# Attention of a two-layer network: turns and products in batches of two groups, with VectorE moving every second group of the selected part

## The chip, the cores and the metric

The kernel runs on one core of a Trainium2 chip. The metric is the time of one execution on the device, in microseconds (us). A core has five engines, each with its own instruction queue, which it works off strictly in order: TensorE (PE; its weight loads are shown as PEld), VectorE (DVE), ScalarE (ACT), GpSimd (POOL) and SyncE (SP). They are tied together by semaphores.

## The reference, cut to what matters

The network has two layers; each is a mixer and a feed-forward block with a convolution. The change touches the mixer of the second layer alone, an attention of 1024 queries and 16 heads of 64 in two groups of keys and values. Each query attends in three ways and the results are added with gates:

```python
s_c = q_blk . k_cmp - slopes * dist_c          
p_c = masked_softmax(s_c, dist_c >= 0)
o_c = p_c . v_cmp
imp = p_c . cover                              # importance of each block of 64 keys
_, top = lax.top_k(imp, 6)                     # first, own and previous block are forced
s_s = q_blk . k_sel[top] - slopes * dist_s     # selected blocks
o_s = masked_softmax(s_s, dist_s >= 0) . v_sel[top]
s_w = q_blk . k_win - slopes * dist_w          # the last 512 keys
o_w = masked_softmax(s_w, valid_w) . v_win
o = g[0] * o_c + g[1] * o_s + g[2] * o_w
```

## The kernel before, in words

The attention is one list, `steps`, of 144 steps (lines 117 to 135). A step is a part (2 compressed, 1 window, 0 selected), a head and a tile of 128 queries. A compressed step does eight heads at once. A window or selected step does two heads against `tiles` tiles of 128 keys: at most 5 in the window, up to 8 in the selected part, where all keys up to the query's tile are scored and the blocks that were not chosen are masked. The first 80 steps are compressed and window steps mixed (16 compressed); they are called the first part. The last 64 steps, from `SELECTED` on, are the selected part. They come in eight couples (two groups of keys, four couples each) of a large and a small query tile: 8 and 1 tiles of keys, 7 and 2, 6 and 3, 5 and 4. Within a couple a wide step and a narrow one take turns, four pairs to a couple.

A step goes through these stages; the names in brackets are the functions:

- TensorE multiplies queries and keys (`scores`, line 1693, matmuls at 1701 and 1711) into PSUM banks 0 to 3. There is room for the scores of one step only, so it first waits until VectorE has read those of the step before (`neg_ready`).
- VectorE adds the mask and slope and takes the extreme (`bias_step`, line 1310, one pass for each of the two heads); compressed steps have their own chain of small operations (`cmp_front`, `cmp_back`).
- ScalarE takes the exponential and its sum (`exp_step`, line 859), VectorE the reciprocal (`norm_step`, line 1321), and GpSimd multiplies by reciprocal and gate (`scale_step`, line 607; semaphore `scaled`).
- TensorE turns the probabilities, block by block of 128 x 128, into bank 4 or 5 (`turn`, line 1735). Up to four blocks, 512 columns, are a group; groups are numbered through all steps (`pair_groups`), 176 in the first part and 160 in the selected part, and group g uses bank 4 + g % 2. A wide and a narrow step have five groups together.
- A group is copied from PSUM into one of five buffers PTR (semaphores `pt_sb` for ScalarE, line 873, and `pt_sv` for VectorE, line 1347).
- TensorE multiplies it with the values (`values`, lines 1748 and 1754) into bank 6 or 7, and VectorE adds the result to the output (`out_step`, lines 1333 and 1335).

The order is fixed by these loops. For step p TensorE first issues the scores of step p + AHEAD, then turns the groups of p one by one, and after each turn of g issues the products of g - LAG; with LAG = 3 and AHEAD = 3 turns and products alternate. VectorE does, for step p, the bias of step p + 3, the reciprocals of step p + 2, and then in `evacuate(p)` goes through the groups of p: copies those that `by_vector` gives it (none before), and does the output sum of a step whose last group is g - LAG. ScalarE does, for step p, the exponentials of step p + 2 and then copies the groups of p. A turn of g waits until group g - 2 has been copied out of its bank:

```python
def turn(g):
    ...
    if g >= 2:
        evacuated(g - 2)
```

The copies by VectorE are written in both kernels; only `by_vector` decides whether there are any:

```python
if by_vector(g):
    w = min(4, tiles - 4 * i) * P
    dve.wait_ge(tr_done, g + 1)
    dve.wait_ge(pv_done, g - len(PTR) + 1)
    dve.tensor_copy(PTR[g % len(PTR)][:, 0:w], PS[:, 4 + g % 2, 0:w]).then_inc(pt_sv, 1)
if ends(g - LAG):
    out_step(group_step[g - LAG])
```

## Time and profile before

| what | before |
|---|---|
| median of three runs | 3404.81 us (3403.2 to 3405.83) |
| the profiled execution | 3404.87 us |
| its span, first to last instruction | 3403.1 us |
| mean granted clock of TensorE | 0.949 |
| TensorE busy | 3063.8 us, 90% |
| GpSimd busy | 1469.3 us, 43% |
| VectorE busy | 1354.4 us, 40% |
| ScalarE busy | 944.9 us, 28% |

The times of a profiled execution are read from the start of its span. Each engine's busy time is what its instructions took; idle time in front of an instruction is given in brackets with the instruction that ended it, or with "issue" where the profile shows nothing that was waited for. A line such as L1735 is a line of the kernel. In the timeline, instructions of one kind that follow each other are merged into one row with their count; a matmul of two passes counts twice, so four products of 64 x 128 appear as x8. The granted clock is the share of TensorE's full clock of 2.4 GHz; 0.50 is 1.2 GHz.

### The profile page before, as it was taken

The page shows a single profiled execution, that of the slowest core. Times are in us where ns is not written, and L with a number is a line of the kernel's source. Part 1 is how long each engine was busy: PE and PEld are TensorE (multiplying, and loading weights), DVE is VectorE, ACT ScalarE, POOL GpSimd, SP SyncE. Part 2 cuts the span into 40 slices and gives each one's busy share as a digit, 9 for nine tenths or more (in the row PEclk, how much of TensorE's full clock was granted, in tenths as well). Part 3 has the DMA queues.
Part 4 walks back from the last instruction along what each step waited for, and adds up shares of the span by engine and source line. Part 5 has one row for each costly group of instructions (what it writes and reads, how often), then busy time and mean ns, then how long its engine had stood idle before and what let it go on. Part 6 is the DMA issues. An engine that isn't in the chain of part 4 may idle for free. (4 is left out here: it accounts for less than half of the span.)

```text
span 3403.1 us, 41503 instructions
## 1 busy us (share of the span) xinstructions
PE 3063.8 (90%) x16565; PEld 2424.3 (71%) x16565; DVE 1354.4 (40%) x1910; ACT 944.9 (28%) x1447; POOL 1469.3 (43%) x910
## 2 busy tenths in 40 slices
PE   5967888977989999999899698889879899999998
PEld 4747887764778888888777465555557688888887
DVE  3675445353333223133300477654342332231334
ACT  3332223222033112012101264667661331120121
POOL 4324433374554444444543243344444544444442
PEclk8988999998999999999899797999989899999999
DMA  3100000110111111111112200000001111111111
GB/s 134 44 25 1 1 1 26 49 50 25 48 33 49 47 46 48 51 49 46 43 44 54 79 2 1 1 1 2 1 13 44 32 49 49 49 48 45 49 46 71
DMA packets 211542, 127.43 MB, mean 37 GB/s; under 512 B 8905, under 2 KB 208078, under 8 KB 211150
## 3 DMA queue, kind: packets, MB, share of 16 engines
q1 hardware_dynamic: 209600, 125.25, 12.5%
q8 instruction: 96, 1.57, 0.2%
q10 hardware_dynamic: 1805, 0.28, 0.0%
q14 instruction: 41, 0.33, 0.0%
HBM read 112.94 MB, written 8.39 MB: 36 GB/s over the span
## 5 line engine op out<-in xcount | busy, mean ns | idle before, releaser
L437 POOL TENSOR_TENSOR WH<-WR,ONES 128x1024 fp32r<-128x1024 f32 (+1 forms) x194 | 459.6, 2369 | 1224.5 <-PE PS L1398 1200.7
L1398 PE MATMUL PS<-YH,WH 128*128 128x512 f32 x2336 | 739.0, 398 | 77.3 <-POOL YL L462 34.7
L1398 PE MATMUL PS<-YL,WH 128*128 128x512 f32 x2336 | 727.2, 393 | 0.0
L1398 PE MATMUL PS<-YH,WL 128*128 128x512 f32 x2336 | 725.5, 392 | 0.0
L1398 PEld LDWEIGHTS PS<-YH,WH 128*128 128x128 f32 x2336 | 441.3, 190 | 192.2 <-issue 53.7
L1398 PEld LDWEIGHTS PS<-YL,WH 128*128 128x128 f32 x2336 | 444.6, 190 | 93.7
L1398 PEld LDWEIGHTS PS<-YH,WL 128*128 128x128 f32 x2336 | 442.6, 189 | 93.2
L440 POOL TENSOR_TENSOR WL<-WR,WH 128x1024 fp32r<-128x1024 f32 (+1 forms) x194 | 482.1, 2485 | 15.2
L1170 DVE SCALAR_TENSOR_TENSOR X<-PS,PTF,X 128x1023 f32<-128x1023 f32 (+1 forms) x176 | 225.7, 1282 | 573.5 <-ACT X L818 560.7
L818 ACT ACTIVATE X<-PS,PTF 128x1024 f32<-128x1024 f32 x88 | 106.2, 1207 | 840.4 <-PE PS L1398 840.2
L873 ACT ACTIVATE Z<-PS 128x512 f32<-128x512 f32 (+2 forms) x336 | 182.6, 545 | 191.6 <-PE PS L1735 189.9
L1398 PE MATMUL PS<-MH,WH 128*128 128x512 f32 x704 | 217.3, 390 | 0.0
L1398 PE MATMUL PS<-MH,WL 128*128 128x512 f32 x704 | 216.9, 389 | 0.0
L1398 PE MATMUL PS<-ML,WH 128*128 128x512 f32 x704 | 216.7, 389 | 0.0
L1711 PE MATMUL PS<-X 64*128 64x512 f32 (+3 forms) x768 | 157.9, 518 | 54.8 <-DVE STAT L1310 54.1
L607 POOL TENSOR_SCALAR X<-X,STAT,SM 128x640 f32<-128x640 f32 (+7 forms) x171 | 135.4, 801 | 144.2 <-DVE STAT L1321 144.2
L1754 PE MATMUL PS<-Z,X 128*64 128x128 f32 x2112 | 188.3, 295 | 9.0 <-DVE Z L1335 9.0
L1754 PEld LDWEIGHTS PS<-Z,X 128*64 128x64 f32 x2112 | 113.3, 140 | 62.4 <-issue 59.5
L1735 PE MATMUL PS<-IDENT,X 128*128 128x128 f32 (+1 forms) x799 | 155.9, 300 | 0.3 <-POOL X L599 0.2
L1398 PEld LDWEIGHTS PS<-MH,WH 128*128 128x128 f32 x704 | 131.9, 188 | 28.9 <-DVE ML L1179 1.6
L1398 PEld LDWEIGHTS PS<-MH,WL 128*128 128x128 f32 x704 | 132.2, 188 | 27.4
L1398 PEld LDWEIGHTS PS<-ML,WH 128*128 128x128 f32 x704 | 132.2, 188 | 27.4
(315 smaller groups left out, 3522.4 us busy)
## 6 DMA issues: line engine op xcount, KB each, us to landing
WR<-in_ffn_w_up_dram SPq DMA_DIRECT2D x88, 512.0 KB, 3.8
WR<-in_hy_w_in_dram SPq DMA_DIRECT2D x28, 512.0 KB, 3.8
WR<-in_ffn_w_down_dram SPq DMA_DIRECT2D x32, 448.0 KB, 3.6
WR<-in_ffn_w_down_dram SPq DMA_DIRECT2D x16, 512.0 KB, 3.8
WR<-in_nsa_w_in_dram SPq DMA_DIRECT2D x14, 512.0 KB, 3.7
Z<-in_x_dram SPq DMA_DIRECT2D x8, 512.0 KB, 7.3
xt_scratch<-H SPq DMA_DIRECT2D x1, 4096.0 KB, 12.1
H<-xt_scratch SPq DMA_DIRECT2D x1, 4096.0 KB, 12.2
```

Of the source, the lines that this page charges most:

```text
L437: pool.tensor_tensor(WH[:, slot, 0:k, :], WR[:, slot, 0:k, :], ONES[:, :].unsqueeze(1).broadcast_to([P, k, P]), ALU.mult).then_inc(w_hi, 1)
L440: pool.tensor_tensor(WL[:, slot, 0:k, :], WR[:, slot, 0:k, :], WH[:, slot, 0:k, :].bitcast(f32), ALU.subtract).then_inc(w_split, 1)
L607: pool.tensor_scalar(score_buf(p, i, 0, w), score_buf(p, i, 0, w), STAT[:, 2, n % 8:n % 8 + 1], GATE[:, qt, gate:gate + 1], ALU.mult, ALU. ...
L818: act.activation(X[:, 16 + s, :], gemm_ps(s), ACT.Identity, scale=PTF[:, bass.ds(j + tap, 1)], bias=PTF[:, bass.ds(j + (C_FBIAS + l * 2 * ...
L873: act.activation(PTR[g % len(PTR)][0:rows, 0:w], PS[0:rows, 4 + g % 2, 0:w], ACT.Copy).then_inc(pt_sb, 1)
L1170: dve.scalar_tensor_tensor(out=X[:, 16 + s, d:], in0=gemm_ps(s)[:, 0:SEQ - d], scalar=PTF[:, bass.ds(j + tap, 1)], in1=X[:, 16 + s, d:], o ...
L1398: ins = pe.matmul(PS[:, 2 * slot + a, :], w[:, slot, i, :], y[:, i, a * HALF:(a + 1) * HALF], start=(i == 0 and w is WH and y is hi), stop ...
L1711: ins = pe.matmul(gemm_ps(i)[:, a:e], X[part, h // 2, chunk(qt)], X[part, kt, first * P + a:first * P + e], start=True, stop=True)
L1735: ins = pe.transpose(PS[0:rows, 4 + g % 2, (k - 4 * i) * P:(k - 4 * i + 1) * P], src, IDENT[:, :])
L1754: ins = pe.matmul(PS[head_part(k), 6 + p % 2, 0:P], X[:, (VS, VW)[b], (first + t) * P + (h // JH) * DH:(first + t) * P + (h // JH) * DH + DH],
```

## The change

```diff
--- before.py
+++ after.py
@@ -145,7 +145,7 @@
         for b_, h_, qt_ in steps:
             pair_groups.append(pair_groups[-1] + (2 if b_ == 2 else (2 * keys_of(qt_, b_)[1] + 3) // 4))
 
-        LAG, AHEAD = 3, 3
+        BATCH, LAG, AHEAD = 2, 2, 3
 
         score_at, scores_free = [], []
         ring, at_ = 0, 0
@@ -173,7 +173,7 @@
         group_step = [p_ for p_ in range(len(steps)) for _ in range(pair_groups[p_], pair_groups[p_ + 1])]
 
         def by_vector(g):
-            return False
+            return group_step[g] >= SELECTED and g % BATCH == 1
 
         n_vector = [sum(by_vector(k) for k in range(g)) for g in range(len(group_step) + 1)]
 
@@ -1759,15 +1759,17 @@
             pe.wait_ge(kv_sb, 2)
             for p in range(AHEAD):
                 scores(p)
-            for p in range(len(steps)):
-                if p + AHEAD < len(steps):
-                    scores(p + AHEAD)
-                for g in range(pair_groups[p], pair_groups[p + 1]):
-                    turn(g)
-                    if g >= LAG:
+            for g0 in range(0, pair_groups[-1] + LAG, BATCH):
+                batch = range(g0, g0 + BATCH)
+                for g in batch:
+                    if g in pair_groups and g < pair_groups[-1] and group_step[g] + AHEAD < len(steps):
+                        scores(group_step[g] + AHEAD)
+                for g in batch:
+                    if g < pair_groups[-1]:
+                        turn(g)
+                for g in batch:
+                    if 0 <= g - LAG < pair_groups[-1]:
                         values(g - LAG)
-            for g in range(pair_groups[-1] - LAG, pair_groups[-1]):
-                values(g)
             pe.wait_ge(y_ready2, MT)
             units(U_NOUT, MT)
             ffn(1, 3, 4 * MT)
```

Three things change. TensorE works in batches of two groups: in a batch it issues the scores of every step that falls due, then both turns, then the products of the two groups before (LAG is 2 now). If both groups of a batch begin a step, two steps' scores stand one after the other at its start. VectorE's output sums stand one group earlier in its queue. And in the selected part VectorE copies the odd groups, 80 of 160, while ScalarE keeps the even ones and all of the first part.

The first place is TensorE in the selected part, in the second kind of couple (7 and 2 tiles of keys). L1711 are scores, L1735 turns of one block each, L1754 products. Before:

```order
L1711 MATMUL PS<-X 128x512 x2
L1711 MATMUL PS<-X 128x384 x2
L1735 MATMUL PS<-IDENT,SRX 128x128 x2
L1754 MATMUL PS<-Z,X 64x128 x4
L1711 MATMUL PS<-X 128x256 x2
L1735 MATMUL PS<-IDENT,SRX 128x128 x4
L1754 MATMUL PS<-Z,X 64x128 x4
L1735 MATMUL PS<-IDENT,SRX 128x128 x4
L1754 MATMUL PS<-Z,X 64x128 x4
L1735 MATMUL PS<-IDENT,SRX 128x128 x4
L1754 MATMUL PS<-Z,X 64x128 x2
```

The same place with the change:

```order
L1711 MATMUL PS<-X 128x512 x2
L1711 MATMUL PS<-X 128x384 x2
L1711 MATMUL PS<-X 128x256 x2
L1735 MATMUL PS<-IDENT,X 128x128 x8
L1754 MATMUL PS<-Z,X 64x128 x6
L1735 MATMUL PS<-IDENT,X 128x128 x8
L1754 MATMUL PS<-Z,X 64x128 x8
L1711 MATMUL PS<-X 128x512 x2
L1711 MATMUL PS<-X 128x384 x2
```

The scores of the wide step (512 and 384 columns) and of the narrow one (256) now stand side by side with no turn or product between them, eight turns come in a row, and then six products.

The second place is VectorE in the selected part, in the first kind of couple (8 and 1 tiles). L1310 is the bias pass, L1321 the reciprocals, L1335 the output sum. Before:

```order
L1310 ISA SRX,STAT<-PS,Z 128x1024 [waits att_sc_ready]
L1310 ISA STAT 128x1
L1321 RECIPROCAL STAT<-STAT 128x2 [waits att_p_ready]
L1310 ISA SRX,STAT<-PS,Z 128x128 [waits att_sc_ready,att_tr_done,att_selb_ready]
L1310 ISA STAT 128x1
L1310 ISA SRX,STAT<-PS,Z 128x128 [waits att_sc_ready]
L1310 ISA STAT 128x1
L1321 RECIPROCAL STAT<-STAT 128x2 [waits att_p_ready]
L1335 TENSOR_TENSOR Z<-Z,PS 128x128 [waits att_o_used,att_pv_done] x2
L1310 ISA X,STAT<-PS,Z 128x1024 [waits att_sc_ready,att_tr_done,att_selb_ready]
```

The same place with the change, where L1347 is the copy of a group:

```order
L1310 ISA SRX,STAT<-PS,Z 128x1024 [waits att_sc_ready]
L1310 ISA STAT 128x1
L1321 RECIPROCAL STAT<-STAT 128x2 [waits att_p_ready]
L1310 ISA SRX,STAT<-PS,Z 128x128 [waits att_sc_ready,att_tr_done,att_selb_ready]
L1310 ISA STAT 128x1
L1310 ISA SRX,STAT<-PS,Z 128x128 [waits att_sc_ready]
L1310 ISA STAT 128x1
L1321 RECIPROCAL STAT<-STAT 128x2 [waits att_p_ready]
L1347 COPY Z<-PS 128x512 [waits att_pv_done,att_tr_done]
L1335 TENSOR_TENSOR Z<-Z,PS 128x128 [waits att_o_used,att_pv_done] x2
L1347 COPY Z<-PS 128x512 [waits att_pv_done,att_tr_done]
```

The first copy stands behind the narrow step's bias and behind reciprocals that wait for ScalarE's exponentials (`att_p_ready`), the second behind two output sums that wait for products (`att_pv_done`).

## Rows read from the trace of the kernel before

**Rows 1.** The profile's page, busy time and share of the span.

```profile
PE 3063.8 (90%) x16565; PEld 2424.3 (71%) x16565; DVE 1354.4 (40%) x1910; ACT 944.9 (28%) x1447; POOL 1469.3 (43%) x910
```

**Rows 2.** Stretches: us, busy time (instructions) by engine, granted clock, DMA share, GB/s.

```profile
1925.00:2050.00 125.00, 116.13 (x1058) 76.48 (x1058) 89.11 (x248) 79.85 (x184) 56.73 (x70) 0.96 0.01 1
2050.00:2135.00 85.00, 69.70 (x496) 45.36 (x494) 60.83 (x139) 35.50 (x83) 27.11 (x31) 0.74 0.00 1
```

**Rows 3.** Timeline, fifth couple: start, length (us), engine, line, work, [idle before <- releaser].

```profile
2401.31 1.99 PE L1711 MATMUL PS<-X 64*128 64x512 f32 x8
...
2403.47 1.23 DVE L1310 CUSTOM_DVE_ANT_0 SRX<-PS,Z 128x1024 f32<-128x1024 f32 x1 [2.93 <-PE PS L1711]
...
2404.74 1.15 ACT L859 ACTIVATE SRX<-SRX,STAT 128x1024 f32<-128x1024 f32 x1 [0.65 <-DVE STAT L1310]
...
2405.90 0.49 PE L1711 MATMUL PS<-X 64*128 64x128 f32 x4 [1.64 <-DVE STAT L1310]
...
2406.32 0.66 PE L1735 MATMUL PS<-IDENT,X 128*128 128x128 f32 x4
...
2407.16 0.17 DVE L1321 RECIPROCAL STAT<-STAT 128x2 f32<-128x2 f32 x1
...
2410.80 1.56 PE L1711 MATMUL PS<-X 64*128 64x512 f32 x6
```

**Rows 4.** Waits, selected part: who waits for whom, us in total, times, longest.

```profile
PEld PS L1711 <- DVE STAT L1310: 26.8, 24, 1.9
```

**Rows 5.** Timeline, third couple, TensorE's matmuls.

```profile
2335.08 0.66 PE L1735 MATMUL PS<-IDENT,X 128*128 128x128 f32 x4
2335.66 0.44 PE L1754 MATMUL PS<-Z,X 128*64 128x128 f32 x4
2336.03 0.66 PE L1735 MATMUL PS<-IDENT,X 128*128 128x128 f32 x4
```

**Rows 6.** Timeline, the last products: TensorE's weight loads.

```profile
2526.66 1.51 PEld L1754 LDWEIGHTS PS<-Z,X 128*64 128x64 f32 x28 [0.17 <-issue]
```

**Rows 7.** Groups by shape, VectorE: xcount | busy us, mean ns | idle before.

```profile
L1262 DVE COPY Z<-PS 128x512 f32<-128x512 f32 x15 | 10.4, 690 | 12.5 <-PE PS L1748 12.3
```

**Rows 8.** Groups by shape, ScalarE, selected part.

```profile
L873 ACT ACTIVATE Z<-PS 128x512 f32<-128x512 f32 x134 | 79.5, 596 | 68.7 <-PE PS L1735 68.5
```

**Rows 9.** Chain of waits: start, length (us), what; one wide step's scores a row.

```profile
2320.76 1.54 PE PS L1711 x8
...
2337.28 1.49 PE PS L1711 x8
...
2352.84 1.28 PE PS L1711 x8
...
2488.66 1.28 PE PS L1711 x8
...
2503.99 1.28 PE PS L1711 x8
```

**Rows 10.** Timeline, first part, TensorE's matmuls.

```profile
1965.40 1.35 PE L1711 MATMUL PS<-X 64*128 64x512 f32 x8
...
1973.30 0.70 PE L1711 MATMUL PS<-X 64*128 64x256 f32 x4 [1.22 <-DVE STAT L1310]
...
1995.15 1.35 PE L1711 MATMUL PS<-X 64*128 64x512 f32 x8
```

**Rows 11.** Timeline, first and second couple, TensorE's matmuls.

```profile
2262.51 1.99 PE L1711 MATMUL PS<-X 64*128 64x512 f32 x8
...
2273.49 1.99 PE L1711 MATMUL PS<-X 64*128 64x512 f32 x8
...
2284.47 1.77 PE L1711 MATMUL PS<-X 64*128 64x512 f32 x8
...
2288.58 0.70 PE L1711 MATMUL PS<-X 64*128 64x256 f32 x4 [1.38 <-DVE STAT L1310]
```

**Rows 12.** Stretches of two us, first couple.

```profile
2270.00:2272.00 2.00, 2.00 (x14) 1.34 (x14) 0.29 (x1) 0.50 (x2) 0.99 (x1) 0.50 0.00 0
```


## The prediction

> **What bounds the kernel now.** I read the page first, then busy time by stretches, the waits and the chain of the attention, and last the timeline, engine by engine. TensorE is busy for 90% of the span [rows 1]. The change acts only on the attention's loop, from 1925 to 2530 us. Its first part (compressed and window steps) lasts to 2246 us, the selected part to 2530 us. In the first part TensorE is near full at the whole clock, and at a mean clock of 0.74 in the 85 us where VectorE ranks the blocks [rows 2]. In the selected part TensorE works steadily and waits for one thing: its next scores stand behind VectorE's passes over the last ones, 26.8 us in all [rows 4]. The fifth couple shows how. Wide scores start at 2401.31 us, VectorE reads them in two passes, and the narrow scores start at 2405.90 us, 4.59 us after the wide ones; 1.64 us of that was idle [rows 3]. The next pair starts 9.49 us after the first.
>
> **What the change removes.** A turn of four blocks takes 0.58 us to the start of the products, products of two blocks 0.37 us [rows 5]. In the tail 28 product loads run without a break in 1.51 us, 0.054 each, so four blocks (8 loads) cost 0.43 us [rows 6]. The rest, 0.15 us, is paid once whenever TensorE goes from turns to products, to scores, or back; the tail's row has 0.17 us of it as idle of the weight loads. A satisfied wait costs nothing visible: that tail passes three groups. Counted over the whole listing of TensorE's instructions, changes of kind fall from 427 to 247 before the first selected turn and from 379 to 211 after it: 348 times 0.155 us is 54 us at most.
>
> This meets a rule that speaks against the change. The Trainium skill, TensorE: Matmul & The Clock Gate, section Step-by-step: what each phase is for, says that the load of the next weights is pulled ahead of running matmuls; by it a change of kind would cost nothing, the saving would be nil, and only the added waits would be left. The trace disagrees, with 0.17 us of idle at each change; the Trainium skill, TensorEngine Tiling (Array Packing), Key Properties, says that changing the tiling mode drains the engine, and that fits.
>
> **What it costs, selected part.** Per step pair there are a wide step (W0, W1, ...) and a narrow one (N...), five groups in all, so batches repeat every two pairs: 5 batches, 10 groups, 36 blocks turned and multiplied. 80 of the 160 groups are now moved by VectorE, 64 of them with 512 columns. Such a copy took 0.69 us from PSUM [rows 7] against ScalarE's 0.60 [rows 8]: about 50 us more for VectorE, which idles for over half of this part. Its length is covered; its place in the queue is not. VectorE copies a step's odd groups only after the bias passes of the step three ahead, the reciprocals of the step two ahead (which wait for ScalarE's exponentials), and the output sum of a step just ended, which waits for its products.
>
> First and fifth couple, eight pairs, wide 8 tiles, narrow 1. Work of two pairs without waits: scores 2 x (1.91 + 0.42), taken from start to start; blocks 72 x 0.1075 = 7.74; ten changes 1.55; together 13.95 us. The waits, with t=0 at the start of the wide scores in the batch that holds N and the next W0:
> - Both scores are now issued at once, so narrow scores start at 4.59 as before [rows 3], with nothing between: 2.68 us idle.
> - N and W0 are turned by 5.8 us. N is even, so ScalarE copies it first (to 5.8) and only then takes the two exponentials of the wide step; from the start of the first to VectorE's reciprocal it was 2.42 us [rows 3], so the reciprocal comes at 8.25. W0's copy stands behind it: done at 9.0. TensorE has done products of four blocks each twice (to 6.8) and the turn of W1 (7.4); the turn of W2 needs W0's bank: 1.6 us idle.
> - In the other batch with wide scores, a turn pair (0.80) and a product pair (1.01) lie between: 4.59 - 1.91 - 1.81 = 0.87 idle. Where the output sum stands ahead of a copy, another 0.3.
> Sum 19.4 us, against 2 x 9.49 = 19.0: longer by 0.45.
> Second and sixth couple, eight pairs (7 and 2 tiles): the same work; narrow scores could start 4.11 us after wide ones of 1.70 [rows 11], so the waits are 2.4, 1.8 (N is four blocks, ScalarE starts later), 0.6 and 0.05: 18.9 against 18.15 (four pairs from 2284.47 [rows 11] to 2320.76 us [rows 9], halved): longer by 0.8.
> Third and seventh (6 and 3 tiles), no two scores in one batch: work 13.7, waits 0.1 and 0.3 for scores, and 1.1 for W0's copy, which now stands behind the output sum of the last wide step, the narrow bias and the reciprocals; with two of 0.1 it is 15.45 against 15.56 [rows 9]. Fourth and eighth (5 and 4): 13.55 + 1.35 + 0.15 = 15.05 against 15.33 [rows 9].
> Each couple kind has four such double pairs: 4 x (0.45 + 0.8 - 0.1 - 0.3) = +3.4 us. Of 26 us of saved changes here nothing is left. Ends: no wait for copies at all, -22 us (the 1.9, 1.85, 1.3 and 1.4 us of them, four times); each of them 0.5 us longer, +12.
>
> **First part.** All copies stay with ScalarE. A cycle of one compressed, two window steps of 5 tiles and a narrow one takes 14.9 us (two in 29.75) with a wait of 1.22 us before the narrow scores [rows 10]. It has nine groups, so nine changes go, 1.4 us. Of the new order I followed two cycles: 24.9 us of work; 1.7 and 1.9 us for narrow scores, since VectorE's work on the compressed step lies ahead of the second wide bias; 0.1 to 0.4 for copies behind exponentials: 28.6 against 29.75, 0.6 less a cycle. Ten cycles at the full clock give 6 us, the rest of the part, where VectorE's ranking or the lower clock rules, 0 to 7, and I take 2: -8 us. Ends: 0, and all 180 changes, -28. The tail (two groups of products fewer) and the start are taken as nothing.
>
> Sum: 3404.87 (profiled; median 3404.81) + 3.4 - 8 = 3400.3, say 3401 us. A measurement of this kernel can tell about 0.2% (6.8 us) from no change; this is inside it.
>
> **The rivals.**
> - The copies come in time. If VectorE's queue is freer than I walked it, the 26 us of its copy waits in the selected part shrink. For it: VectorE was under half busy there; against: the queue is in order, and the wide exponentials of 2.4 us cannot be hidden by 1.6 us of work. Three quarters gone: 3400 - 19 = 3381 us. The Trainium skill, TensorEngine Tiling (Array Packing), PSUM Bottleneck, advises ScalarE and VectorE together for emptying PSUM; by it this rival is the natural outcome.
> - The longer single waits pull TensorE's clock. In the first couple a wait of 1.64 us was followed by a stretch at 0.50 of the clock (1.2 GHz) [rows 12], and that pair took 10.98 us [rows 11] against 9.49: 1.5 us. In the fifth couple the same wait did nothing. Now eight double pairs have waits of 2.4 to 2.7 and then 1.6 to 1.8 us. If each drops it, 8 x 1.5 = 12 us more, less the some 3 us already paid in the first couple, with 3 more in the first part: 3401 + 12 = 3413 us. It decides from about half of them on.
> - The change does nothing: no; the listing shows the batches and 80 copies.
>
> **How the numbers follow.** Forecast 0.45 (it reaches about 8 us to either side: faster 0.12, same 0.30, slower 0.03), copies in time 0.30 (faster), clock 0.25 (same 0.08, slower 0.17). Faster 0.42, same 0.38, slower 0.20. The range takes in the middle of the first rival and the second's whole: 3382 to 3414.
>
> **What would show it.** Wide scores followed at once by narrow ones, with idle of 2.4 to 2.7 us for VectorE's STAT in the first, second, fifth and sixth couples; TensorE's turns (line 1735 of before) waiting 1 to 2 us for VectorE's copy, about 20 us in all, where they waited for no copy; fewer 0.17 us idles; double pairs of 19.4, 18.9, 15.4 and 15.1 us; the first part about 8 us shorter. It is wrong if turns wait for VectorE's copy for under 10 us, if the first part moves by over 15 us, or if the clock of the four slow couples falls below 0.85.

## The result, and the profile after

| what | before | after |
|---|---|---|
| median of six runs each, same chip | 3405.61 us | 3419.99 us (3419.49 to 3421.83) |
| the profiled execution | 3404.87 us | 3419.88 us |
| its span | 3403.1 us | 3418.1 us |
| mean granted clock of TensorE | 0.949 | 0.948 |

The ratio after to before is 1.0046, 95% interval 1.0035 to 1.0056. The change made the kernel slower by 14 us. The forecast was 3401 us with a range of 3382 to 3414, so the result lies outside it, on the slower side.

The busy times of the kernel after, to be read against [rows 1]:

```profile
PE 3032.7 (89%) x16565; PEld 2438.5 (71%) x16565; DVE 1397.8 (41%) x1990; ACT 890.1 (26%) x1367; POOL 1470.3 (43%) x910
```

VectorE has its 80 copies (1990 instructions against 1910) and 43 us more work, ScalarE 80 fewer and 55 us less. TensorE has the same 16565 matmuls and 31 us less busy time, in a program that is 15 us longer: what grew is idle time of TensorE.

The length of the selected part, from VectorE's first bias of 1024 columns to the first operation of ScalarE on the attention's sum (line 883), went from 280.6 us (2248.22 to 2528.79) to 296.7 us (2246.24 to 2542.95). The first part, from 1925 us to that bias, went from 323.2 to 321.2 us. So the selected part lost 16.1 us, the first part gained 2.0, and these two nearly make up the difference of the profiled executions.

The table sets the eight couples of the selected part side by side, from wide bias to wide bias: length in us, and the mean granted clock behind the stroke.

| couple | 1 | 2 | 3 | 4 | 5 | 6 | 7 | 8 |
|---|---|---|---|---|---|---|---|---|
| before | 38.2 / 0.91 | 36.0 / 1.00 | 31.9 / 1.00 | 31.5 / 1.00 | 36.4 / 1.00 | 36.0 / 1.00 | 31.9 / 1.00 | 38.7 / 1.00 |
| after | 36.0 / 1.00 | 40.6 / 0.92 | 34.0 / 0.95 | 32.3 / 1.00 | 41.6 / 0.92 | 38.8 / 0.96 | 33.9 / 0.95 | 39.5 / 1.00 |

**The waits.** These are the waits of the selected part in the kernel after: us in total, times, longest. The first row answers to [rows 4].

```profile
PEld PS L1711 <- DVE STAT L1310: 43.5, 32, 3.4
...
PE PS L1711 <- DVE STAT L1310: 32.9, 28, 2.6
...
PEld PS L1735 <- issue: 27.1, 66, 0.8
PEld PS L1735 <- DVE Z L1347: 22.1, 23, 2.2
...
PE PS L1735 <- DVE Z L1347: 16.5, 18, 1.9
...
DVE STAT L1321 <- ACT SRX L859: 12.2, 7, 2.4
...
DVE STAT L1321 <- ACT X L859: 8.3, 5, 2.3
```

The same wait has a row of the weight loads (PEld) and one of the matmuls (PE); the first is the larger, and the two are not to be added. Of the kernel before the matmuls' row for the maximum is

```profile
PE PS L1711 <- DVE STAT L1310: 21.3, 20, 1.6
```

Sums of waits below are those of the weight loads where nothing else is said; waits read from a timeline of TensorE's matmuls are the matmuls'. Scores wait for VectorE's maximum 43.5 us, against 26.8 us before. Turns now wait 22.1 us for VectorE's copy (line 1347), of which there was none before. The "issue" idle in front of turns, in which the changes of kind lie, is 27.1 us in 66 places; before it was 41.5 us in 141. In front of products it went from 27.8 us (162) to 12.7 us (76).

**One double pair.** This is the timeline of the fifth couple in the kernel after, TensorE and VectorE, to be read against [rows 3]:

```profile
2408.55 1.99 PE L1711 MATMUL PS<-X 64*128 64x512 f32 x8
2410.70 1.23 DVE L1310 CUSTOM_DVE_ANT_0 SRX<-PS,Z 128x1024 f32<-128x1024 f32 x1 [2.38 <-PE PS L1711]
...
2413.14 0.49 PE L1711 MATMUL PS<-X 64*128 64x128 f32 x4 [2.60 <-DVE STAT L1310]
2413.56 1.17 PE L1735 MATMUL PS<-IDENT,X 128*128 128x128 f32 x6
...
2414.66 1.98 PE L1754 MATMUL PS<-Z,X 128*64 128x128 f32 x16
...
2416.71 0.17 DVE L1321 RECIPROCAL STAT<-STAT 128x2 f32<-128x2 f32 x1 [2.07 <-ACT X L859]
2416.79 0.69 DVE L1347 COPY Z<-PS 128x512 f32<-128x512 f32 x1
...
2421.64 1.23 DVE L1310 CUSTOM_DVE_ANT_0 X<-PS,Z 128x1024 f32<-128x1024 f32 x1 [2.14 <-PE PS L1735]
...
2424.07 0.49 PE L1711 MATMUL PS<-X 64*128 64x128 f32 x4 [1.32 <-DVE STAT L1310]
```

The narrow scores start 4.59 us after the wide ones, as forecast, with 2.60 us of idle in front, since nothing stands between. The two turns of the batch (six blocks) end by 2414.7 us, but the copy of the second starts at 2416.79 us: VectorE stood 2.07 us at a reciprocal that waited for ScalarE's exponentials. And at 2421.64 us a thing is to be seen that the forecast didn't have: VectorE starts a wide bias only when TensorE has done turns (its releaser is line 1735, not 1711), because the buffer it writes is still being turned. The narrow scores behind it wait 1.32 us instead of the 0.87 us forecast.

TensorE's clock around that wait, in stretches of two us (columns as in [rows 2]):

```profile
2413.00:2415.00 2.00, 1.86 (x14) 1.41 (x16) 0.67 (x7) 0.97 (x2) 0.88 (x2) 0.75 0.00 0
2415.00:2417.00 2.00, 2.00 (x18) 1.67 (x15) 0.29 (x2) 1.67 (x4) 0.03 (x1) 0.50 0.00 0
2417.00:2419.00 2.00, 2.00 (x22) 1.41 (x20) 1.06 (x4) 0.60 (x1) 2.00 (x2) 0.90 0.00 0
```

Behind the wait of 2.60 us about 3.4 us passed at half the clock (1.2 GHz): (0.25 + 0.50 + 0.10) x 2 us x 2. The products in it, sixteen rows, took 1.98 us, and 1.09 us at the full clock seven us later.

The chain of waits of the kernel after gives the wide scores of the fifth to eighth couples, one row each, to be read against [rows 9]:

```profile
2398.65 2.82 PE PS L1711 x8
...
2419.00 1.92 PE PS L1711 x8
...
2439.02 1.70 PE PS L1711 x8
...
2458.92 1.70 PE PS L1711 x8
...
2478.54 1.49 PE PS L1711 x8
...
2495.14 1.54 PE PS L1711 x8
...
2511.34 1.28 PE PS L1711 x8
...
2527.08 1.28 PE PS L1711 x8
```

Double pairs took 20.35, 19.90, 16.60 and 15.74 us; forecast were 19.4, 18.9, 15.45 and 15.05.

**The first part.** Compressed scores (line 1701) mark its cycles. First before, then after, TensorE's timeline:

```profile
1930.42 1.25 PE L1701 MATMUL PS<-X 64*128 64x63 f32 x16
...
1990.81 1.11 PE L1701 MATMUL PS<-X 64*128 64x63 f32 x16
...
2139.51 1.11 PE L1701 MATMUL PS<-X 64*128 64x63 f32 x16
...
2169.03 1.11 PE L1701 MATMUL PS<-X 64*128 64x63 f32 x16
```

```profile
1928.54 1.46 PE L1701 MATMUL PS<-X 64*128 64x63 f32 x16
...
1958.69 0.80 PE L1711 MATMUL PS<-X 64*128 64x128 f32 x4 [4.17 <-DVE STAT L1310]
...
1996.23 1.11 PE L1701 MATMUL PS<-X 64*128 64x63 f32 x16
...
2133.26 1.11 PE L1701 MATMUL PS<-X 64*128 64x63 f32 x16
...
2166.69 1.11 PE L1701 MATMUL PS<-X 64*128 64x63 f32 x16
```

The first five intervals between compressed scores took 60.4 us before and 67.7 after, the next eight 148.7 and 137.0, the last two 29.5 and 33.4. So the middle gained 11.7 us and the two ends lost 11.2. The loss at the start has a wait of 4.17 us. The scores of a wide and of a narrow window step stand side by side there, and VectorE has its operations on a compressed step (lines 1243 to 1249) ahead of the wide bias. The kernel before had 0.64 us in front of the same narrow scores. The granted clock tells the same: from 1925 to 1985 us it was 0.92 before and is 0.82 now, from 2135 to 2200 us it was 1.00 and is 0.92, and from 2050 to 2135 us it rose from 0.74 to 0.82.

### The profile page after: what moved, and what is told of

It is laid out like the page before. It is cut to its first block, busy times and chain, and to the rows that moved or that the text cites. A ratio compares the mean times of both kernels' runs of the same rounds, so it can differ in the third digit from the quotient of the medians.

```text
span 3418.1 us, 41503 instructions
## 1 busy us (share of the span) xinstructions
PE 3032.7 (89%) x16565; PEld 2438.5 (71%) x16565; DVE 1397.8 (41%) x1990; ACT 890.1 (26%) x1367; POOL 1470.3 (43%) x910
## 3 DMA queue, kind: packets, MB, share of 16 engines
q1 hardware_dynamic: 209600, 125.25, 12.4%
## 4 chain that ended last, share of the span: by engine, by line
PE 74%; DVE 15%; ACT 3%; POOL 3%; issue 2%; DMA 1%; SPq 0%; ACTq 0%; DVEq 0%; POOLq 0%
PE PS L1398 55%; PE PS L1711 4%; PE PS L1735 3%; PE PS L1476 3%; PE PS L1754 2%; DVE X L1310 2%; DVE H L962 2%; POOL YL L462 1%; DVE X L947 1%; PE PS L1534 1%; DVE SRX L1310 1%; DVE X L910 1%; DVE X L1074 1%; DVE X L924 1%; POOL YL L531 1%
## 5 line engine op out<-in xcount | busy, mean ns | idle before, releaser
L440 POOL TENSOR_TENSOR WL<-WR,WH 128x1024 fp32r<-128x1024 f32 (+1 forms) x194 | 482.0, 2485 | 15.2
L1711 PE MATMUL PS<-X 64*128 64x512 f32 (+3 forms) x768 | 160.8, 526 | 86.3 <-DVE STAT L1310 82.4
L607 POOL TENSOR_SCALAR X<-X,STAT,SM 128x640 f32<-128x640 f32 (+7 forms) x171 | 135.6, 802 | 167.5 <-DVE STAT L1321 167.5
L873 ACT ACTIVATE Z<-PS 128x512 f32<-128x512 f32 (+2 forms) x256 | 132.9, 539 | 268.8 <-PE PS L1735 267.8
L1711 PEld LDWEIGHTS PS<-X 64*128 64x128 f32 x768 | 68.5, 200 | 151.4 <-DVE STAT L1310 100.9
L1754 PE MATMUL PS<-Z,X 128*64 128x128 f32 x2112 | 160.5, 292 | 5.1 <-DVE Z L1262 2.3
L1735 PE MATMUL PS<-IDENT,X 128*128 128x128 f32 (+1 forms) x799 | 140.2, 298 | 12.7 <-DVE Z L1347 11.5
```

The costliest lines, as they stand in the source:

```text
L440: pool.tensor_tensor(WL[:, slot, 0:k, :], WR[:, slot, 0:k, :], WH[:, slot, 0:k, :].bitcast(f32), ALU.subtract).then_inc(w_split, 1)
L607: pool.tensor_scalar(score_buf(p, i, 0, w), score_buf(p, i, 0, w), STAT[:, 2, n % 8:n % 8 + 1], GATE[:, qt, gate:gate + 1], ALU.mult, ALU. ...
L873: act.activation(PTR[g % len(PTR)][0:rows, 0:w], PS[0:rows, 4 + g % 2, 0:w], ACT.Copy).then_inc(pt_sb, 1)
L1711: ins = pe.matmul(gemm_ps(i)[:, a:e], X[part, h // 2, chunk(qt)], X[part, kt, first * P + a:first * P + e], start=True, stop=True)
L1735: ins = pe.transpose(PS[0:rows, 4 + g % 2, (k - 4 * i) * P:(k - 4 * i + 1) * P], src, IDENT[:, :])
L1754: ins = pe.matmul(PS[head_part(k), 6 + p % 2, 0:P], X[:, (VS, VW)[b], (first + t) * P + (h // JH) * DH:(first + t) * P + (h // JH) * DH + DH],
```

## The experiments

The theory after the result: the saving of changes of kind is real, and is given back by two things, (a) scores of two steps side by side, and (b) VectorE's copies behind the rest of its queue. The rival: the falls of TensorE's clock behind the longer single waits take the time. Times are medians of 4 to 10 executions, ratios are to the kernel before on the same chip with their 95% interval. Lengths of parts and waits are those of one profiled execution each; in experiments 4 and 12 that execution was about 4 us shorter than the median.

**1. The batches alone, ScalarE copies everything.**

```diff
 def by_vector(g):
-    return group_step[g] >= SELECTED and g % BATCH == 1
+    return False
```

> The changed kernel, but ScalarE copies every group. Theory A (VectorE's copies stand behind its bias passes, reciprocals and output sums, and TensorE's turns wait for them): the 38.7 us of waits for VectorE's copy go, ScalarE's copies wait behind exponentials instead, since in a batch the copy of the second group has 2.0 us and the wide exponentials alone take 2.3: some 20 to 30 us of waits for ScalarE. Time 3410 to 3420 us. Rival B (VectorE as such was the fault and ScalarE has room): under 3400 us. Rival C (ScalarE is the worse place): over 3425 us.

Measured: 3407.82 us, 1.0010 (1.0001 to 1.0020). Selected part 284.5 us. Of the change's 14 us, 12 go with VectorE's copies, more than the 10 us at most that were expected. What is left is still no gain: the waits for the maximum stay at 43.1 us, and waits for ScalarE's copies have taken the place of VectorE's 22.1 us:

```profile
PEld PS L1735 <- ACT Z L873: 19.7, 24, 1.8
```

So the 12 us can't be read from the row of the copies: turns wait for ScalarE nearly as long as for VectorE. In the account below idle fell by 9.1 us, 6.2 of it in the "issue" rows, for which the trace names no reason, and the time at half clock went from 24 to 14 us. (The expectation's 38.7 us of waits for VectorE's copy comes out only if the 22.1 us of the weight loads and the 16.5 of the matmuls are added, which counts the same waits twice; so with the 39 us in the expectation of experiment 5.)

**2. VectorE's copies alone**, in the kernel before, without batches.

```diff
 def by_vector(g):
-    return False
+    return group_step[g] >= SELECTED and g % 2 == 1
```

> The kernel before, its order of turns and products kept, with VectorE copying every odd group of the selected part. Theory A: with turns and products in alternation a copy has longer before its bank is wanted, but the first odd group of a wide step still stands behind bias, reciprocals and exponentials; some waits for the copy, selected part longer by 0 to 8 us: 3403 to 3413 us. Rival B (the copies by themselves make the whole loss): 3418 us or more. Rival C (the loss comes from the batches alone): within 2 us of the kernel before.

Measured: 3406.83 us, 1.0009 (0.9999 to 1.0019). Selected part 284.5 us in its profile, waits for line 1347 of 4.7 us in front of turns and 3.2 in front of products. The same copies that cost 12 us in batches cost 2 to 3 here, hardly to be told from none. That the copies have less room in batches, where two turns follow each other and the batch after needs both banks at once, fits this and is argued only.

**3. LAG of 2 alone**, in the kernel before.

```diff
-LAG, AHEAD = 3, 3
+LAG, AHEAD = 2, 3
```

> The kernel before with products two groups behind the turn instead of three, nothing else. Every theory: the number of changes of kind stays, VectorE's output sums stand one group earlier. I expect no difference above 2 us; if it is slower by over 5 us, the smaller distance and not the batch makes part of the loss.

Measured: 3407.28 us, 1.0006 (0.9996 to 1.0015); selected part 281.0 us. The smaller lag costs nothing that can be told from none.

**4. The second step's scores behind the first turn.** In the kernel after, the loops over a batch for scores and for turns are made one.

```diff
 for g in batch:
     if g in pair_groups and g < pair_groups[-1] and group_step[g] + AHEAD < len(steps):
         scores(group_step[g] + AHEAD)
-for g in batch:
     if g < pair_groups[-1]:
         turn(g)
```

> The changed kernel, but the scores of a batch's second step stand after the turn of its first group, not beside the other scores. Theory A (adjacent scores leave TensorE idle for all of VectorE's two passes and delay the turn, ScalarE's copy and the exponentials behind it): N is turned 2.7 us earlier, ScalarE starts its exponentials earlier, and of each double pair of the first, second, fifth and sixth couples 1 to 2.5 us come back, with three more changes of kind; 8 double pairs: 8 to 16 us, time 3404 to 3412 us. If the clock follows the length of a single wait (theory C) its falls in these couples go as well. Rival B (the waits for VectorE's copies alone matter): no change over 3 us.

Measured: 3400.15 us, 0.9985 (0.9975 to 0.9994). Selected part 278.4 us against 296.7. One turn between the two scores gives back 20 us, more than the 8 to 16 expected. The idle in front of the narrow scores of the fifth couple is 2.23 us instead of 2.60: the turn fills only a part of it, but it is done that much earlier, and its copy and the next exponentials with it. In all, waits for the maximum fell to 32.2 us and those for VectorE's copy to 17.3.

**5. Copies ahead of the reciprocals.** In the kernel after, VectorE goes through a step's groups first in the selected part, and takes the reciprocals of the step two ahead behind them.

```diff
-if p + AHEAD - 1 < len(steps):
+if p + AHEAD - 1 < len(steps) and p < SELECTED:
     norm_step(p + AHEAD - 1)
...
+if p >= SELECTED and p + AHEAD - 1 < len(steps):
+    norm_step(p + AHEAD - 1)
```

> The changed kernel, but in the selected part VectorE takes a step's copies and output sums before the reciprocals of the step two ahead, so no copy stands behind an exponential. Theory A (the copy waits behind the reciprocals, which wait for ScalarE's exponentials): the waits for VectorE's copy fall from 39 us to under 20, 1 to 1.5 us less a double pair, 16 of them: 3395 to 3408 us. Rival B (the copy is held by the output sum and the bias, not by the reciprocals): under 4 us of gain. Against both, the reciprocals now come later and GpSimd's scaling with them; if turns then wait for GpSimd it is no faster or slower.

Measured: 3405.50 us, 0.9998 (0.9989 to 1.0008). Selected part 278.7 us. Nothing but the place of one small instruction a step (0.16 us) was changed, and all of the change's 14 us came back. The waits of its selected part (line numbers are two higher below the edit):

```profile
PEld PS L1737 <- DVE Z L1347: 11.5, 14, 1.5
```

Half of the 22.1 us are gone, and of the 20.5 us that VectorE's reciprocals stood waiting for exponentials in the kernel after 0.2 are left. So about half of the lateness of VectorE's copy came from the reciprocal in front of it, and not from VectorE's speed. A part of the gain may be the clock's: only two falls were left in the selected part, of seven, though all eight waits of 2.07 to 2.60 us in front of narrow scores were still there, and idle fell by 13.0 us where the part became 18.0 shorter. No run separates the two.

**6. TensorE kept busy between adjacent scores.** In the kernel after, ten needless products of 128 x 128 stand between the two scores of a batch, in a bank that is free; they compute nothing that is used.

```diff
+due = [g for g in batch if ...]
+for g in due:
+    scores(group_step[g] + AHEAD)
+    if len(due) == 2 and g == due[0] and group_step[g] >= SELECTED:
+        evacuated(g0 - 2)
+        for _ in range(10):
+            pe.matmul(PS[:, 4 + g0 % 2, 0:P], IDENT[:, :], IDENT[:, :], start=True, stop=True)
```

> The changed kernel with ten needless 128 x 128 products between adjacent scores of the selected part, in the idle time of 2.4 to 2.7 us there, written to the bank of turned blocks that is free then. Nothing waits less. Theory C (a single long wait lowers TensorE's clock and the stretch at half clock behind it is dear): the falls in the first, second, fifth and sixth couples go, 5 to 7 of them at 1.5 to 1.9 us: 3407 to 3412 us, clock 1.00 in all those couples. Rival (the waits themselves are the whole loss): 3419 to 3421 us. If ten products are too long for the gap, later by up to 0.5 us a double pair: the trace shows the next scores' wait gone.

Measured: 3417.79 us, 1.0034 (1.0023 to 1.0046). In all eight couples the granted clock was 1.00, so the falls were taken away whole, and the selected part was 292.3 us long, 4.4 less. The narrow scores of the fifth couple still start 4.59 us after the wide ones, so the needless products delay nothing there. By the ratios the kernel gained 4 us and by the medians 2, and the two intervals overlap. The clock explains about 4 us of what the change lost there, and by the intervals not more than some 9. That is less than the 8 to 13 us expected if the clock were dear, and more than the nothing expected if the waits were all. Why it is not more is seen in the timeline of the fifth couple, kept busy:

```profile
2409.27 0.88 PE L1735 MATMUL PS<-IDENT,X 128*128 128x128 f32 x6
2410.07 1.09 PE L1754 MATMUL PS<-Z,X 128*64 128x128 f32 x16
2411.10 0.66 PE L1735 MATMUL PS<-IDENT,X 128*128 128x128 f32 x4
2413.24 0.66 PE L1735 MATMUL PS<-IDENT,X 128*128 128x128 f32 x4 [1.49 <-DVE Z L1347]
```

At the full clock turns and products are done sooner (the products in 1.09 us instead of 1.98), and then the next turn waits 1.49 us for VectorE's copy. By the weight loads it is 1.72 us, where the same turn had 0.26 in the kernel after. Summed over the selected part that wait grew from 22.1 to 27.8 us. In this pair most of what the half clock had cost was time that would have passed in a wait anyway. The clock of the first part, at half for 73 us in the kernel after and for 64 before, was not touched by this run.

**7. Both cures: scores apart, ScalarE copies everything.** The edits of experiments 4 and 1.

> Scores apart as in e4_scores_apart (3400.2 us), but ScalarE copies every group. With adjacent scores the same step from VectorE to ScalarE gave 12 us. If those 12 us were VectorE's place in the queue in general, it gives as much here: about 3388 us. If they came from adjacent scores plus clock falls that are gone here already, 3396 to 3402 us. Over 3404 us would mean that ScalarE's exponentials now hold the copies more than VectorE's queue did.

Measured: 3389.58 us, 0.9946 (0.9927 to 0.9965). Selected part 266.6 us, 14.0 less than in the kernel before. This is the 3388 us that was expected if the 12 us were VectorE's place in the queue in general. The two costs nearly add: VectorE's copies cost 12 us with adjacent scores (experiment 1) and 11 with the scores apart (from 3400.15), adjacent scores 20 us (experiment 4) and 18 (from 3407.82). Without both the batches do gain.

**8. Scores apart, copies by VectorE ahead of the reciprocals.** The edits of experiments 4 and 5.

> Scores apart and, in the selected part, VectorE's copies ahead of the reciprocals. Theory A: the 17 us of waits for VectorE's copies in e4_scores_apart fall by half or more: 3388 to 3396 us, the best of all. Rival: the reciprocals are late for GpSimd and TensorE's turns wait for the scaling instead: 3400 us or more.

Measured: 3397.68 us, 0.9977 (0.9968 to 0.9987). Selected part 277.2 us; waits for line 1347 fell only from 17.3 to 14.4 us. The move that gave 14 us beside adjacent scores gives 2.5 here. The time lies between the two expectations. With the turn between the scores the reciprocals in front of a copy hold it for far less already: VectorE stood 2.4 us at them in experiment 4, against 20.5 in the kernel after. Copies by VectorE still stand behind bias passes and output sums, and cost 8 us against ScalarE's (experiment 7). That these two are what holds them is argued from the queue; no run moved them.

**9. Second scores at the end of the batch**, ScalarE copies everything.

```diff
+for g in due[:1]:
+    scores(group_step[g] + AHEAD)
 for g in batch:
     ...
         turn(g)
 for g in batch:
     ...
         values(g - LAG)
+for g in due[1:]:
+    scores(group_step[g] + AHEAD)
```

> Batches of two, copies all on ScalarE, and the scores of a batch's second step stand behind both products of the batch instead of behind its turns' end. Against the kernel with ScalarE's copies and the scores apart, 3389.6 us (0.9946 of the kernel before). Theory 1 (what the batch lost came from adjacent scores only, and any work between the two scores cures it): two turns and two products now stand between a batch's scores, the waits for the maximum in the selected part fall from about 32 us to 15 or less, and the time is 3380 to 3389 us, 0.992 to 0.9945. Rival 2 (the loop bias, maximum, exponentials, normalising, copy sets the pace once scores come late): later scores make the exponentials and so the next turn late; the waits of products for copies or of turns for normalised values grow by as much, and the time is 3390 to 3410 us.

Measured: 3385.10 us, 0.9930 (0.9911 to 0.9948). Selected part 263.8 us; the narrow scores of the fifth couple wait 0.77 us. Waits for the maximum fell to 25.5 us and not to the 15 expected, and waits for ScalarE's copies grew (20.0 us in all against 10.5). The time is the first theory's, the growth of those waits the rival's: more work between the scores is better, but the loop through copy and exponentials takes part of it back.

**10. Experiment 7 with LAG 3.**

```diff
-BATCH, LAG, AHEAD = 2, 2, 3
+BATCH, LAG, AHEAD = 2, 3, 3
```

> The kernel with batches, ScalarE's copies and the second scores behind the first turn (3389.6 us, 0.9946 of the kernel before), with the scores three steps ahead of the products instead of what it had. Theory 1 (what is left in it are the turns' changes of kind and the copies, about 10 us of waits for ScalarE's copies in the selected part): a larger lead of the scores moves no copy earlier relative to its product, the copies' waits stay, and the time is within 3 us of 3389.6. Rival 2 (the 32 us of waits for the maximum are what is left): with more work between a step's scores and its exponentials they fall below 20 us and the time is 3380 to 3386 us.

Measured: 3402.71 us, 0.9992 (0.9983 to 1.0002), 13 us slower than experiment 7. Both expectations missed it. (The expectation's opening speaks of scores three steps ahead; what was changed is LAG, the products three groups behind the turns instead of two.) The waits of its selected part:

```profile
DVE Z L1335 <- PE PS L1754: 80.4, 51, 5.2
...
PEld PS L1711 <- DVE STAT L1310: 39.3, 32, 2.5
```

Experiment 7 had 52.3 us in the first of these rows and 31.8 in the second. The timeline of the third couple with LAG 3 shows how they are tied:

```profile
2335.55 1.56 PE L1711 MATMUL PS<-X 64*128 64x512 f32 x8
...
2338.34 0.29 DVE L1335 TENSOR_TENSOR Z<-Z,PS 128x128 f32<-128x128 f32 x1 [2.97 <-PE PS L1754]
2338.54 0.95 DVE L1310 CUSTOM_DVE_ANT_0 X<-PS,Z 128x768 f32<-128x768 f32 x1
...
2340.44 0.92 PE L1711 MATMUL PS<-X 64*128 64x384 f32 x4 [1.34 <-DVE STAT L1310]
```

The scores are done by 2337.2 us. VectorE stands at an output sum that waits for a product one group later than with LAG 2, and starts the bias 1.3 us late; the next scores wait 1.34 us for it. In experiment 7 the same scores (at 2333.47 us there) wait for nothing. LAG 2 alone was worth nothing (experiment 3); in batches it is worth 13 us. It is part of what makes them pay. Only half of it is seen here: the selected part is 6.6 us longer than in experiment 7 and the first part 6.3, which was not followed up.

**11. Second scores between turns and products**, ScalarE copies everything. As experiment 9, with the loop over `due[1:]` ahead of the products.

> Batches of two, ScalarE copies everything, and the second scores of a batch stand between its turns and its products. Neighbours: adjacent scores 3407.8 (1.0010 of the kernel before), second scores behind the first turn 3389.6 (0.9946), behind turns and products 3385.1 (0.9930). Theory 1 (it counts how much work stands between the two scores, and whether the copy of the turned groups is reached in time): both turns stand between, 0.8 to 1.1 us against a wait of about 2.7, and the copies of the batch get the scores as further cover; the waits for the maximum in the selected part are near 30 us, those for ScalarE's copies below 10, and the time is 3384 to 3391 us. Rival 2 (scores that come behind the turns make VectorE's bias wait for the turns, as in the kernel where they stand last, which had 33 us of such waits, and this sets the time): as much of such waits and 3388 to 3400 us.

Measured: 3378.96 us, 0.9915 (0.9897 to 0.9933), 27 us below the kernel before and 41 below the change, and the fastest of all; better than either theory expected. Selected part 266.3 us, first part 310.9. The page's busy times:

```profile
PE 3016.2 (89%) x16565; PEld 2429.5 (72%) x16565; DVE 1354.5 (40%) x1910; ACT 925.7 (27%) x1447; POOL 1470.7 (44%) x910
```

and the waits of its selected part:

```profile
PEld PS L1711 <- DVE STAT L1310: 32.8, 32, 2.0
...
DVE X L1310 <- PE PS L1735: 25.6, 12, 3.2
```

The second row is the one of the rival: the waits of VectorE's bias for turns are there, as large as in experiment 1 (26.1 us), and the kernel is 29 us faster all the same. Such a wait marks a bias that comes late, but it isn't what the adjacent scores cost. The selected part is as in experiment 7; the further gain is in the first part, where the eight cycles in the middle took 135.6 us and the last two 28.1 (1993.83, 2129.44 and 2157.56 us are the starts), and the clock of 2135 to 2200 us was 0.97 against 0.92 in the kernel after.

**12. The change in the first part alone**, single groups with LAG 2 behind it, ScalarE copies everything.

```diff
+whole = range(g0, g0 + BATCH)
+for batch in ([whole] if g0 < pair_groups[SELECTED] else [[g] for g in whole]):
```

> The change in the first part alone: batches of two before the selected part, single groups with LAG 2 behind it, ScalarE copies everything. Theory 1 (the change's loss arises in the selected part, its first part gains 2 us by the stage lengths read from the two traces; LAG 2 alone in the selected part costs nothing that can be told from none, 1.0006): first part 319 to 323 us long, selected part 280 to 283, time within 3 us of the kernel before (0.999 to 1.001). Rival 2 (the first part's gain of 8 us was real and is given back at the border or by the lower clock that the selected part's waits leave behind): 3395 to 3399 us, 0.997 to 0.9985.

Measured: 3402.90 us, 0.9988 (0.9979 to 0.9998), with a first part of 319.7 us and a selected part of 277.7 in its profile (323.2 and 280.6 in the kernel before). That is 3 us of gain by the medians and 4 by the ratio, with an interval that ends at 7. The time is nearer to the first theory than to the rival's 3395 to 3399, the ratio lies between them; the forecast's 8 us are just excluded.

**The account.** For each kernel the length of the selected part and what TensorE's weight loads stood idle for in it, us. The last column also has the "issue" idle in front of scores, 20 to 21 us in every row.

| kernel | length | maximum | copies | "issue", turns and products | all idle |
|---|---|---|---|---|---|
| before | 280.6 | 26.8 | 2.7 | 69.3 | 120.1 |
| after | 296.7 | 43.5 | 24.1 | 39.8 | 128.0 |
| 1 ScalarE copies | 284.5 | 43.1 | 22.4 | 33.6 | 118.9 |
| 4 scores apart | 278.4 | 32.2 | 17.9 | 43.9 | 114.2 |
| 5 copies first | 278.7 | 43.5 | 12.4 | 39.2 | 115.0 |
| 7 apart, ScalarE | 266.6 | 31.8 | 10.5 | 39.6 | 102.1 |
| 9 scores last | 263.8 | 25.5 | 20.0 | 35.7 | 101.8 |
| 10 LAG 3 | 273.2 | 39.3 | 4.5 | 44.8 | 108.4 |
| 11 between | 266.3 | 32.8 | 14.8 | 36.3 | 103.9 |

From before to experiment 7 idle fell by 18.0 us and the part by 14.0; from before to after idle rose by 7.9 and the part by 16.1. For the kernel after, the rest can be work at the lower clock: by the table of couples it spent 23 us at half clock (2 x (1 - clock) x length, summed) and the kernel before 7, which is at most 8 us of work done slower. For experiment 7, with 10 us at half clock, that gives less than 2 of the 4 us; the others are not traced. The count of falls differs between the runs too: seven in the kernel after, four, three and two in experiments 1, 4 and 5. What share of the gains of these three is the clock's isn't separated; experiment 6, with all seven gone, bounds it.

## Why the prediction was wrong

- **The saving of changes of kind** was right. Forecast for the selected part were 26 us; the "issue" idle in front of turns and products fell by 29.5 us over 161 fewer places, 0.18 us each against the 0.155 taken. The Trainium skill, TensorE: Matmul & The Clock Gate, section Step-by-step: what each phase is for, has the next weights loaded while a matmul runs, where the row groups do not conflict or the load goes to the background buffer. Taken without these conditions, as the prediction took it, it would have the saving at nothing; the trace has 0.18 us a change. Experiment 7 turns 14 us of it into time.
- **Turns waiting for VectorE's copy**: forecast about 20 to 26 us, measured 22.1 (16.5 in the matmuls' row). The mechanism was right too: a reciprocal in front of the copy, and experiment 5, which moves it, takes half of the wait away.
- **The step that failed: the scores' waits for the maximum.** The forecast's waits, set against those of the trace before, are 3.55 us a double pair against 3.28, 3.0 against 2.76, and 0.4 against 1.78 in the third kind; they come to no increase. (The 3.28 are twice 1.64 us. Only the last two pairs of the first and of the fifth couple waited that long before; the first two waited 0.25 us, and the sum took 9.49 us for each pair of them too.) Measured were 43.5 us against 26.8, 16.7 more; in the matmuls' rows, by which the forecast's waits were taken, 32.9 against 21.3, 11.6 more. By kinds of couple, from the first to the fourth, the weight loads' waits grew by 4.9, 4.8, 3.9 and 3.0 us. Three things were missing. VectorE's bias waits until the buffer that it writes has been turned, and turns come later in batches, so the second wait is 1.32 us instead of 0.87. In the first pair of the third and seventh couples two scores still stand side by side, with 2.07 us of wait, where I had walked the later pairs alone. And the first narrow scores of the first and fifth couple wait 0.77 to 1.10 us where it was 0.25. The waits of 0.21 to 0.55 us in the fourth kind, where there were none before, weren't in the forecast either. Experiment 4 shows the size: apart, the scores give 20 us back. Its waits for the maximum are 11 us shorter and those for copies 6, its changes of kind cost 4 us more, and it has four falls of the clock fewer.
- **Double pairs** came 0.95, 1.0, 1.15 and 0.7 us longer than forecast. Four times that is 15.2 us; with the +3.4 it would be +18.6, and +16.1 was measured. Of the 19 us between the forecast of 3401 and the result 13 lie in the selected part and 6 in the first.
- **First part**: forecast -8, measured -2.0, and -3.5 in the profile of experiment 12. Two cycles came out at about 29.3 us instead of 28.6, and the ends, which I took as gaining, lost 11 us, with the wait of 4.17 us and the lower clock shown above. Experiment 11 has 28.54 us for the two cycles from 1993.83 us: the forecast cycle exists, with the scores elsewhere.
- **Rival 1, the copies in time**: no. The copies' waits stayed whole. The Trainium skill, TensorEngine Tiling (Array Packing), PSUM Bottleneck, advises to share the emptying of PSUM between ScalarE and VectorE; here it cost 12 us in batches and 2 to 3 without. Experiment 5, which changes only the order in VectorE's queue, got 14 us back, so the place in the queue decided here.
- **Rival 2, the clock**: half right. Falls came in five couples instead of one, seven in all, six of them behind waits of 2.07 to 2.60 us and one behind 1.10; a wait of 2.60 us in the first couple and one of 2.33 in the sixth were followed by none. Its price of 12 us was too high: experiment 6 took every fall away and got about 4 us. None of the couples was below the 0.85 that I had set as proof.
- The range ended at 3414. Its upper end was made of the clock alone, as if the walked waits were sure. The end of +12 us that the copies' waits had been given, with the first part at nothing, would have reached 3417; a bound for the waits for the maximum was not given at all, and that was the term that moved.

## What to carry to other kernels

Grouping instructions to save on changes of an engine's mode pays only if what is grouped isn't waiting for another engine: keep between two dependent instructions as much independent work as they had before, here the scores of two steps with turns or products between them (29 us lie between experiments 1 and 11, which differ only in where the second scores stand). Work given to an idle engine arrives when its queue lets it: read what stands in front of it and what that waits for, and move waiting instructions behind it first. When an order is changed, walk every buffer that the producers write, not only the ones that the edit names.

## What the runs showed of the hardware

- A wait of 2.60 us of TensorE was followed by 3.4 us at half the clock, and yet taking all seven such falls away, 24 us in all, was worth about 4 us, where 12 would be the most. In the pair that was followed, the half-clock work ran in the shade of another wait (1.72 us at the full clock, 0.26 at the half).
- The same eight waits of 2.07 to 2.60 us stand in the selected part of the kernel after and of experiments 1 and 5, and the clock fell behind six, four and two of them: a wait of this length alone did not decide.
- VectorE's copy of 128 x 512 from PSUM took 0.68 us in the selected part, over 64 of them, as the 0.69 of [rows 7]: the engine was as fast as taken, so the loss of 12 us did not come from slower copies than forecast.
